# Weight tiles at offset addresses in a two-layer decoder trunk on one Trainium2 core: the high halves begin 32 bytes further, the low halves 96

## The reference

```python
for i in range(DEPTH):
    z = rmsnorm(h, norm_mix_pre[i])
    z = mlstm_mixer(z, ...) if i % N_MIXERS == 0 else swa_sink_mixer(z, ...)
    h = h + rmsnorm(z, norm_mix_post[i])
    z = conv_ffn(rmsnorm(h, norm_ffn_pre[i]), f_w_up[i], f_conv_w[i], f_conv_b[i], f_w_down[i])
    h = h + rmsnorm(z, norm_ffn_post[i])

def conv_ffn(h, w_up, conv_w, conv_b, w_down):
    gate, val = jnp.split(h @ w_up, 2, axis=-1)
    gate_c = conv_b + sum(conv_w[j] * gp[:, j:j + S] for j in range(CONV_W))   # gp: gate padded in front
    return (jax.nn.silu(gate_c) * val) @ w_down
```

## The kernel before

| tensor | before | in the change |
|---|---|---|
| `raw`, `act_hi`, `act_lo`, `h`, `g_post`/`g_pre` (`t_third`), `arena` (`t_early`, `hid`, `zn`) | 0 | 0 |
| `w_hi` | 0 | 32 |
| `w_lo`, `sums` | 0 | 96 |
| `hid_pair`, high and low | 0 | 64 |
| `t_last`, `t_last_sum` | 64 | 0 |
| `ident` (the moving operand of transposes) | 32 | 32 |

## Time and profile before

### The profile page before, as it was taken

The page is one execution under the profiler, slowest core; times in us unless marked ns, Lnnn a source line. Parts: engine busy times, 40 slices in busy tenths (PEclk is TensorE's granted clock), DMA queues, the critical chain, the costliest instruction groups (busy, mean ns, idle before and its releaser), DMA issues.

```text
span 1060.2 us, 18750 instructions
## 1 busy us (share of the span) xinstructions
PE 1051.5 (99%) x6822; PEld 943.5 (89%) x6822; DVE 730.1 (69%) x1013; ACT 531.5 (50%) x971; POOL 271.9 (26%) x195
## 2 busy tenths in 40 slices
PE   9999999999999999999999999999999999999997
PEld 8888888898999999988889987789999999988886
DVE  7534579588988988633366577678898898943354
ACT  6511447445565565422355367754566566542242
POOL 1000211004565565100000023300656556400000
PEclk9999999999999999999999999999999999999999
DMA  9342328233343343122272552123234334222232
GB/s 287 108 120 80 100 81 253 48 97 91 89 119 109 88 119 113 55 92 97 99 198 61 133 127 80 21 60 100 64 96 119 100 98 119 79 80 99 99 139 80
DMA packets 154828, 111.18 MB, mean 105 GB/s; under 512 B 35536, under 2 KB 140144, under 8 KB 154784
## 3 DMA queue, kind: packets, MB, share of 16 engines
q1 hardware_dynamic: 153776, 107.41, 34.5%
q0 software_dynamic: 864, 2.92, 0.9%
q10 hardware_dynamic: 144, 0.26, 0.1%
HBM read 106.87 MB, written 2.13 MB: 103 GB/s over the span
## 4 chain that ended last, share of the span: by engine, by line
PE 93%; DVE 4%; SPq 1%; ACT 1%; issue 1%; DMA 0%; DVEq 0%; ACTq 0%
PE ps L2061 11%; PE ps L2063 11%; PE ps L2062 11%; PE ps L2095 8%; PE ps L2096 8%; PE ps L2094 8%; PE ps L1808 6%; PE ps L1810 5%; PE ps L1809 5%; PE ps L2000 2%; PE ps L2002 2%; PE ps L2001 2%; PE ps L1889 1%; PE ps L1890 1%; PE ps L1891 1%; PE ps L2191 1%
## 5 line engine op out<-in xcount | busy, mean ns | idle before, releaser
L1808 PE MATMUL ps<-act_hi,w_hi 128*128 128x256 f32 (+1 forms) x440 | 144.8, 329 | 1.5 <-DVE act_lo L1153 1.4
L1809 PE MATMUL ps<-act_lo,w_hi 128*128 128x256 f32 (+1 forms) x440 | 142.4, 324 | 0.0
L1810 PE MATMUL ps<-act_hi,w_lo 128*128 128x256 f32 (+1 forms) x440 | 142.4, 324 | 0.0
L2061 PE MATMUL ps<-act_hi,w_hi 128*128 128x256 f32 x432 | 122.4, 283 | 0.0
L2062 PE MATMUL ps<-act_lo,w_hi 128*128 128x256 f32 x432 | 122.4, 283 | 0.0
L2063 PE MATMUL ps<-act_hi,w_lo 128*128 128x256 f32 x432 | 122.4, 283 | 0.0
L1604 DVE TENSOR_TENSOR w_lo<-raw,w_hi 128x1024 fp32r<-128x1024 f32 x32 | 39.2, 1225 | 117.0 <-ACT w_hi L952 117.0
L611 POOL TENSOR_TENSOR sums<-raw 128x512 f32<-128x512 f32 x36 | 48.3, 1341 | 262.3 <-PE ps L1810 139.6
L2095 PE MATMUL ps<-w_lo,w_hi 128*128 128x512 f32 x288 | 112.1, 389 | 0.0
L2094 PE MATMUL ps<-w_hi 128*128 128x512 f32 x288 | 112.1, 389 | 0.0
L2096 PE MATMUL ps<-w_hi,w_lo 128*128 128x512 f32 x288 | 112.1, 389 | 0.0
(11 more groups left out here) (267 smaller groups left out, 2839.6 us busy)
## 6 DMA issues: line engine op xcount, KB each, us to landing
raw<-in_f_w_up SPq DMA_DIRECT2D x88, 512.0 KB, 4.6
raw<-in_f_w_down SPq DMA_DIRECT2D x44, 512.0 KB, 3.2
raw<-in_m_w_in SPq DMA_DIRECT2D x23, 512.0 KB, 4.2
raw<-in_m_w_out SPq DMA_DIRECT2D x8, 512.0 KB, 3.3
raw<-in_a_w_in SPq DMA_DIRECT2D x16, 256.0 KB, 4.5
raw<-in_a_w_out SPq DMA_DIRECT2D x16, 256.0 KB, 4.7
h<-in_x SPq DMA_DIRECT2D x4, 512.0 KB, 7.9
h<-in_x_turned SPq DMA_DIRECT2D x3, 512.0 KB, 6.7
```

The costliest lines, as they stand in the source:

```text
L1808: nc.tensor.matmul(dst, uh[:, k], zh, start=(k == 0), stop=False)
L1809: nc.tensor.matmul(dst, uh[:, k], zl, start=False, stop=False)
L1810: ins = nc.tensor.matmul(dst, ul[:, k], zh, start=False, stop=(k == KT - 1))
L2061: nc.tensor.matmul(dst, uh, zh, start=(start and k == 0), stop=False, skip_group_check=not start)
```

## The change

Four unused pads are allocated, which shift `w_hi` by 32 bytes and `w_lo` by 96 (modulo 128), bring the activations back to 0, and `t_last` from 64 to 0. `hid_pair` moves by 8 elements within `w_hi` and by 24 within `w_lo`, which puts both at 64; it now reaches 8 and 24 elements into slot 3, so that `freed` makes later users of slot 3 wait, as those of slot 2 did, for the last pair of layer 0. In every product the two operands' starts then differ by 32 or 96 bytes modulo 128: in `project` and `product` moving less stationary is -32 for the two matmuls with `w_hi` and -96 (that is +32) for the one with `w_lo`; in `v_unit` and `out_part` it is +32 and +96 (-32); in `down_part` 32 - 64 = -32 and 96 - 64 = +32, or with the tail in `act_hi` +32 and +96.

No engine's instructions, their order or their number change, and no semaphore that an instruction waits for; only addresses do, and the wait values of the slot 3 units.

```diff
+    SKEW = 8
...
     def freed(g):
         users = [q for q in range(g) if SLOT[q] == SLOT[g]]
-        if SLOT[g] == 2 and g > G_DOWN[0]:
+        if SLOT[g] in (2, 3) and g > G_DOWN[0]:
             users.append(G_DOWN[0] + FT - TAIL - 1)
...
         raw = sb("raw", [P, 4, D])
+        sb("skew", [P, SKEW])
         w_hi = sb("w_hi", [P, 8, D], F32R)
+        sb("lo_skew", [P, 2 * SKEW])
         w_lo_at = below()
         w_lo = sb("w_lo", [P, 8, D], F32R)
         sums = nc.alloc_sbuf_tensor_at("sums", [P, 2, 8, D // 2], F32, offset=w_lo_at)
+        sb("unskew", [P, SKEW])
         act_hi = sb("act_hi", [P, KT, S], F32R)
...
         parts = sb("parts", [P, 3, S // 2])
+        sb("t_skew", [P, 2 * SKEW])
         t_last_at = below()
         t_last = sb("t_last", [P, 2, D], F32R)
...
-        hid_pair = [[w[:, 2, j * HALF:(j + 1) * HALF] for w in (w_hi, w_lo)] for j in range(2)]
+        h0 = 2 * D
+        hid_pair = [[w[:].rearrange("p s c -> p (s c)")[:, h0 + o * SKEW + j * HALF:h0 + o * SKEW + (j + 1) * HALF]
+                     for w, o in ((w_hi, 1), (w_lo, 3))] for j in range(2)]
```

## The result

The change makes the kernel slower: 1075.88 us in the median of 4 runs (1075.86 to 1076.61) against 1062.05 for the kernel before on the same chip; the ratio is 1.0133, interval 1.0118 to 1.0148. I had forecast 1034.

A forecast was written before the change was run, and what follows sets the result against it. PE, busy 99% of the span, was taken as the bound, so matmul pitch counts. Gains of 7.1 + 12.6 + 9 = 28.7 us off 1061.99 gave 1033.3, with 0.3 for the median 1034; range 1023 to 1050.

The forecast's parts named there:

- The nearest row is 64 bytes, 6.7 ns saved, and I take that: All float32r products: differences of 32 or 96 bytes would save 6.7 ns a matmul, as read from `t_last` at 64.
- when they begin at the same place modulo 128: SBUF reads: the next matmul's weight load and this one's stream get in each other's way, costing up to 6.7 ns.
- the term of the down-projection: Down-projection: 1056 matmuls at 6.7 ns saved, 7.1 us, all of it counted.
- that of the rest: Other projections: 2008 matmuls at 6.7 ns are 13.4 us, of which 9 us count because chains outside PE hide some.
- the units' term: Units of seven: period falls from 10.00 to 9.65 us, 0.35 us in each of 36 units, 12.6 us gained.
- A preference for one sign would average out: Every product: two matmuls of one sign mix with one of the other, so the sign of the difference was costed at nothing.
- Slower: only 64 bytes help: Units of seven: 32 and 96 conflict like 0, `t_last` loses its gain; 2.9 us slower, 1065; chance 0.12.
- More: All products: more saved than at 64 bytes, pitch near 110 ns, 36.6 us off, 1025; chance 0.13.
- full: All products: full effect, 5 to 8 ns saved a matmul, 1029 to 1041; chance 0.50.
- half: All products: half the effect, 32 bytes give 3.3 ns a matmul, 15.4 us off, 1047; chance 0.18.
- the limit of 9.65 us by VectorE's chain: Units of seven: VectorE's chain and its mutual blocking with GpSimd keep a unit's period from falling below 9.65 us.
- Costing VectorE's splits at nothing: VectorE's splits at new addresses: no cost in the sum; 2% slower in the units would be 6.5 us, left to the range.

The follow-up runs named there:

- table: Not the trunk: TensorE alone streams float32r matmuls, 96 per pair of start addresses; 113.3 to 120.0 ns at 256 columns, 226.7 to 234.3 at 512.
- hid32: Kernel before, with only the down-projection's stationary tiles in `hid_pair` moved by 32 bytes (864 matmuls); 1067.60 us, ratio 1.0043.
- both32_hid: `both32` with the down-projection's stationary hidden activations at 32 bytes as well, like the weights; 1070.52 us.
- all64: Changed kernel with other offsets: both weight halves start at 64 bytes, everything else TensorE reads with them at 0; 1066.79 us, ratio 1.0047.
- both32: Changed kernel with other offsets: both weight halves start at 32 bytes, activations and `hid_pair` at 0; 1076.99 us, ratio 1.0143.
- both96: Changed kernel with other offsets: both weight halves start at 96 bytes, activations and `hid_pair` at 0; 1067.27 us, ratio 1.0047.
- t64: Kernel before, with `t_early` and `t_third` shifted by 64 bytes, as `t_last` already is; 1060.88 us, ratio 0.9991.
- forms64: Kernel before, with `t_last` at 0 and the weight forms of the units of seven shifted by 64 bytes; 1057.71 us, ratio 0.9958.
- tlast0: Kernel before, with `t_last` alone moved from 64 to 0 bytes; 1064.98 us, ratio 1.0031.
- forms8: Kernel before, with `t_last` at 0 and the weight forms of the units of seven shifted by 8 bytes; 1052.01 us, ratio 0.9899.
- table2: Not the trunk: matmul streams alone, differences 4 to 120 bytes entered from difference 0, some from 32; 64 bytes at 256 columns ran at 113.3 or 117.8 ns.

## Why the prediction was wrong

**Right:** what bounds the kernel, and that all of the effect would be pitch. The mechanism in its barest form, that the difference of the operands' starts moves the pitch, is shown by `table`, by `hid32` and by `both32_hid`. The Trainium skill's rule (SBUF — State Buffer, "Who interferes with whom"), that TensorE's two read ports are independent, by which nothing should have changed, does not cover this: a stream with no other engine at work runs at 226.7 or 233.3 ns by the start address alone. That TensorE doesn't wait for other engines agrees with the long products: the down-projection runs at 226.7 and 233.3 ns with VectorE and ScalarE at work, as the streams alone do. The units of seven in the changed kernel don't settle it, 120.0 ns against 117.8 for the same mixture alone.

**The step that failed** is "The nearest row is 64 bytes, 6.7 ns saved, and I take that", applied to all 6088 matmuls. It joined two extrapolations. The first is from 256 columns to 512. I had worked out one surcharge, 13.3 ns, and concluded that both shapes would lose the same part of it; but the working takes the price of the columns from the difference of the two pitches, so that it must give both shapes the same surcharge, and says nothing of whether an address moves both. In `all64` the down-projection at 64 bytes costs 233.3 ns, 6.6 ns more than at 0; difference 0 is bad for 256 columns and as good as any measured for 512. So the reason that I gave, that two reads collide "when they begin at the same place modulo 128", is refuted for 512 columns. At the change's 32 bytes the long products pay the same 233.3, which turns the term of the down-projection from -7.1 to +7.0 us and that of the rest from -9 to +3.9. The second is from 64 bytes to 32 and 96: in the units these gave 120.0 ns in the mean, in the changed kernel's mixture, where I took 113.3; the units' term is +2.9 in place of -12.6. "A preference for one sign would average out" was an assumption without a row: 32 alone costs 120.0 ns in the units (`both32`) and 96 alone 117.7 (`both96`), and their mixture 120.0, not the mean.

**A third error, which the first two hid:** I read 113.3 ns off `t_last` as the pitch of 64 bytes. It is one of two patterns at that difference. `t64`, `forms64` and `all64` land in the other, 117.5 to 117.9 ns, and in that pattern 64 bytes in all products of a unit give 84 x 2.1 ns = 0.18 us, less the 0.08 that `t_last` had already brought: the 9.90 us of `all64`, where I had reckoned with a pitch worth 9.52.

**The rivals.** "Slower: only 64 bytes help" had the time of the units (10.08 us, 2.9 us), and `tlast0` confirms what `t_last` is worth, but the 1065 it gave lacks the loss of the long matmuls. Its condition is wrong as well: 96 bytes alone (`both96`) and 8 bytes (`forms8`) help the units; 32 alone (`both32`) and the mixture of the change land on 120.0. Its last sentence, a worse conflict at 2 ns a matmul, 1077, comes within 1.2 us of the result by luck: 13.8 us less the 2.9 of `t_last` are 1.8 ns over 6088 matmuls, but the loss isn't spread over them; it sits in the 2248 of 512 columns. "More", "full" and "half" fall together.

**Not reached:** the limit of 9.65 us by VectorE's chain. `forms8` ends at 9.71, just above, so it stays an untested reading. Costing VectorE's splits at nothing was right in its effect: the 65 that one line makes kept their 1219 ns (L1103 before, L1110 after); the first split of a unit, which takes turns with GpSimd, went from 1762 ns in the mean (L1520) to 1867 (L1527), but a unit took the 84 x 120 ns of its matmuls, so PE never waited for it.

**Open:** why a stream settles in one pattern or the other, why the mixture of 32 and 96 takes 120.0 ns in the units and 117.8 alone, and why `t_last` found 113.3 in the kernel before with the moving tile at 64, where the same pair in `table2`, also entered from difference 0, ran at 117.8. The trunk changes its tiles with each matmul and has other engines at work, and the tables do neither; no run here separates that. Nor does any run test that the addresses count modulo 128: the streams cover differences below 128 bytes.

## What to carry to other kernels

A row measured in one shape prices that shape: before carrying it to another number of columns, measure a stream of that shape alone, which takes one short kernel for many offsets. It shows which offsets are worth a trial, not what they bring: `table` had 113.3 ns for 64 bytes and the trunk 117.9. Where a matmul stream is dense and TensorE is the bound, the start addresses of stationary and moving tiles are worth such a table, and an offset belongs only on the products that gain: here 8 bytes on the tiles of 256 columns made 1% and 32 and 96 bytes on all weight tiles cost 1.3%. Judge by the pitch in the timeline, not by the durations of matmuls or weight loads.

## What the runs showed of the hardware

The pitch of float32r matmuls moves with the difference of the operands' start addresses: from 113.3 to 121.7 ns at 256 columns, from 226.7 to 234.3 at 512, in streams of one pair of addresses (the 121.7 at 24 bytes, in `table2`). Many of these streams settle in a cycle that repeats for tens of matmuls (229, 232, 226 ns for 512 columns at 64 bytes in `table2`), and the same pair can have more than one settled value (113.3 and 117.8 ns at 256 columns and 64 bytes). The Trainium skill's isolated gap of a single warm matmul (TensorE: Matmul & The Clock Gate, "Back-to-back issue gap"), N / 2.4 + 2.5 ns, gives estimates of 109.2 and 215.8; no float32r stream here came nearer than 4.1 and 10.9 ns to them.
